# Five raw places and three high places for streamed weight tiles, in place of four and four

## What is computed

```
gate, up = split(rms_norm(h, g_ffn_pre) @ w_ffn_in, 2)            # stack 1
h = h + rms_norm((silu(gate) * up) @ w_ffn_out, g_ffn_post)
x = x + 0.5 * swiglu_ffn(rms_norm(x, ffn1_norm[i]), ffn1_w_in[i], ffn1_w_out[i])   # stack 2
```

## Time and profile before

| | us |
|---|---|
| median of 3 runs | 2286.14 (2285.11 to 2287.39) |
| the profiled execution's own time | 2287.08 |
| its span, first to last instruction | 2285.3 |
| TensorE busy | 2260.3 (99%) |
| TensorE's weight loads | 1985.0 (87%) |
| VectorE busy | 1577.3 (69%) |
| ScalarE busy | 1317.1 (58%) |
| weights' DMA queue, share of 16 engines | 52.5% |

### The profile page before, as it was taken

One profiled execution on the slowest core, in us unless ns is written; L12 is line 12 of the kernel. 1 busy time (PEld: TensorE's weight loads), 2 busy tenths in 40 slices (PEclk: granted clock), 3 DMA queues, 4 the chain that ended last, 5 costly groups with the idle time before them and its releaser, 6 DMA issues.

```text
span 2285.3 us, 31183 instructions
## 1 busy us (share of the span) xinstructions
PE 2260.3 (99%) x13072; PEld 1985.0 (87%) x13072; DVE 1577.3 (69%) x1803; ACT 1317.1 (58%) x1797; POOL 39.0 (2%) x74
## 2 busy tenths in 40 slices
PE   8999999999999999999999999999999999999998
PEld 8898888878988888888898889888888898989886
DVE  6866767478766775667577767675776588667755
ACT  6665655477655655565448745554554558555544
POOL 1000000010000000010000000000100000000000
PEclk9999999999999999999999999999999999999999
DMA  7615555556245655566555355555665655455553
GB/s 227 227 65 184 185 193 188 183 189 231 96 148 184 203 185 193 184 203 193 184 181 178 119 191 191 196 187 186 200 208 177 202 167 166 142 191 183 186 193 120
DMA packets 323515, 411.92 MB, mean 180 GB/s; under 512 B 11600, under 2 KB 245456, under 8 KB 323376
## 3 DMA queue, kind: packets, MB, share of 16 engines
q1 hardware_dynamic: 318160, 394.68, 52.5%
q0 software_dynamic: 4928, 14.26, 2.1%
q10 hardware_dynamic: 288, 0.99, 0.1%
HBM read 408.85 MB, written 1.05 MB: 179 GB/s over the span
## 4 chain that ended last, share of the span: by engine, by line
PE 88%; DVE 5%; ACT 4%; DMA 1%; issue 1%; SPq 0%; DVEq 0%; ACTq 0%
PE banks L610 27%; PE banks L618 14%; PE banks L687 9%; PE banks L689 9%; PE banks L688 9%; PE banks L594 3%; PE banks L595 3%; PE banks L596 3%; DVE lo L1769 2%; ACT hi L1185 1%; DMA raw<-in_w_in 1%; PE banks L738 1%; PE banks L864 1%; PE banks L873 1%; PE banks L841 1%
## 5 line engine op out<-in xcount | busy, mean ns | idle before, releaser
L1769 DVE TENSOR_TENSOR lo<-raw,hi 128x2048 fp32r<-128x2048 f32 (+1 forms) x382 | 858.4, 2250 | 521.9 <-ACT hi L1185 518.0
L1185 ACT ACTIVATE hi<-raw 128x2048 fp32r<-128x2048 f32 (+1 forms) x382 | 715.7, 1878 | 254.3 <-DMA raw<-in_ffn_w_out 84.5
L610 PE MATMUL banks<-x_in,hi 128*128 128x512 f32 x2304 | 537.7, 390 | 0.0
L610 PEld LDWEIGHTS banks<-x_in,hi 128*128 128x128 f32 x2304 | 427.7, 188 | 86.1 <-issue 0.4
L618 PEld LDWEIGHTS banks<-x_in,lo 128*128 128x128 f32 x2304 | 286.5, 192 | 5.8 <-issue 0.2
L618 PE MATMUL banks<-x_in,lo 128*128 128x256 f32 x2304 | 289.3, 283 | 0.0
L594 PE MATMUL banks<-x_in,hi 128*128 128x256 f32 x736 | 210.5, 286 | 0.0
L595 PE MATMUL banks<-x_in,hi 128*128 128x256 f32 x736 | 208.2, 283 | 0.0
L596 PE MATMUL banks<-x_in,lo 128*128 128x256 f32 x736 | 208.2, 283 | 0.0
L687 PE MATMUL banks<-hi,x_hid 128*128 128x512 f32 x528 | 206.0, 390 | 0.0
L689 PE MATMUL banks<-hi,x_hid 128*128 128x512 f32 x528 | 205.5, 389 | 0.0
(11 more groups left out here) (343 smaller groups left out, 3081.0 us busy)
## 6 DMA issues: line engine op xcount, KB each, us to landing
raw<-in_w_in SPq DMA_DIRECT2D x108, 1024.0 KB, 5.1
raw<-in_ffn_w_in SPq DMA_DIRECT2D x88, 1024.0 KB, 5.1
raw<-in_w_ffn_in SPq DMA_DIRECT2D x44, 1024.0 KB, 5.1
raw<-in_ffn_w_out SPq DMA_DIRECT2D x40, 1024.0 KB, 5.1
raw<-in_w_ffn_out SPq DMA_DIRECT2D x20, 1024.0 KB, 5.1
raw<-in_w_o_gla SPq DMA_DIRECT2D x8, 1024.0 KB, 5.2
raw<-in_w_o_attn SPq DMA_DIRECT2D x8, 1024.0 KB, 5.2
raw<-in_w_out SPq DMA_DIRECT2D x8, 1024.0 KB, 5.1
```

The source lines that it names most:

```text
L610: mm = pe.matmul(bank[b + f], wh[:, k, f * P:(f + 1) * P], x[:, k, :, :].rearrange("p n s -> p (n s)"), start=(start and k == 0), stop=(k ...
L1185: act_fn(high, of, ACT.Copy).then_inc(hi_done.up(), 1)
L1769: tt(rest, of, parts(tile, hi)[0].bitcast(F32), ALU.subtract).then_inc(lo_done.up(), 1)
```

## The change

The raw places (with the remainders in them) become five, the high places three, with the same 64 KB together. So a load waits for the tile five before it, and each `hi` index is taken modulo three. ScalarE gets a wait of its own before it writes a high part: for the tile three before to be used. Nothing else moves, and the number of instructions differs only by these waits.

```
-SLOTS = 4
+SLOTS, HIGHS = 5, 3
...
-        o_hi, o_raw = room(SLOTS * 8 * KB), room(SLOTS * 8 * KB)
+        o_hi, o_raw = room(HIGHS * 8 * KB), room(SLOTS * 8 * KB)
...
-        hi = [at(f"hi{i}", [P, TILE], o_hi + i * 8 * KB, F32R) for i in range(SLOTS)]
+        hi = [at(f"hi{i}", [P, TILE], o_hi + i * 8 * KB, F32R) for i in range(HIGHS)]
...
+        def high_slot(tile):
+
+            return place(tile) % HIGHS
...
-                wh = hi[slot(tile)][:, 0:tile.kc * cols].rearrange("p (k n) -> p k n", k=tile.kc)
+                wh = hi[high_slot(tile)][:, 0:tile.kc * cols].rearrange("p (k n) -> p k n", k=tile.kc)
...
                     tile = layer_tiles[0][made[0]]
                     act.wait_ge(*landed(tile))
+                    if place(tile) >= HIGHS:
+                        act.wait_ge(*tile_used.at(tile.index + 1 - HIGHS))
```

More of the change, by code:

```diff
@@ L401, in ranks @@
         def ranks(tile, of, part, twin):
-            dims = of[slot(tile)][:, 0:tile.kc * P].rearrange("p (k d g l r) -> p k d g l r", k=tile.kc, d=2, g=2, l=2)
+            dims = of[place(tile) % len(of)][:, 0:tile.kc * P].rearrange("p (k d g l r) -> p k d g l r", k=tile.kc, d=2, g=2, l=2)
             return dims[:, :, :, twin, part, :]
@@ L421, in parts @@
             if tile.nc >= P:
-                return of[slot(tile)][:, 0:tile.kc * tile.nc], as_loaded(tile)
+                return of[place(tile) % len(of)][:, 0:tile.kc * tile.nc], as_loaded(tile)
             src = as_loaded(tile).rearrange("p (k n) -> p k n", k=tile.kc)
-            return (of[slot(tile)][:, 0:tile.kc * P].rearrange("p (k c n) -> p k c n", k=tile.kc, n=tile.nc),
+            return (of[place(tile) % len(of)][:, 0:tile.kc * P].rearrange("p (k c n) -> p k c n", k=tile.kc, n=tile.nc),
                     src.unsqueeze(2).broadcast_to([P, tile.kc, P // tile.nc, tile.nc]))
@@ L604, in joint_b @@
                 take(b, b + 1)
-                wh = hi[slot(tile)][:].rearrange("p (k n) -> p k n", k=KD)
+                wh = hi[high_slot(tile)][:].rearrange("p (k n) -> p k n", k=KD)
                 wl = lo[slot(tile)][:].rearrange("p (k n) -> p k n", k=KD)
@@ L667, in rows_a @@
             def rows_a(tile, x, to, t, first, last, late=None, turn=None):
-                wh = hi[slot(tile)][:, 0:tile.kc * tile.nc].rearrange("p (k n) -> p k n", k=tile.kc)
+                wh = hi[high_slot(tile)][:, 0:tile.kc * tile.nc].rearrange("p (k n) -> p k n", k=tile.kc)
                 wl = lo[slot(tile)][:, 0:tile.kc * tile.nc].rearrange("p (k n) -> p k n", k=tile.kc)
@@ L792, in ple_rows @@
                     pe.wait_ge(*lo_done.at(tile.index + 1))
-                wh = hi[slot(tile)][:, 0:TILE].rearrange("p (k n) -> p k n", k=2)
+                wh = hi[high_slot(tile)][:, 0:TILE].rearrange("p (k n) -> p k n", k=2)
                 wl = lo[slot(tile)][:, 0:TILE].rearrange("p (k n) -> p k n", k=2)
@@ L893, in low_rank @@
                 take(b)
-                w = hi[slot(tile)][:, 0:tile.kc * P].rearrange("p (k n) -> p k n", k=tile.kc)
+                w = hi[high_slot(tile)][:, 0:tile.kc * P].rearrange("p (k n) -> p k n", k=tile.kc)
                 for k in range(tile.kc):
```

## The result

The changed kernel takes 2303.61 us (median of 4 runs, 2302.31 to 2303.96) where the kernel before took 2285.7 beside it: a ratio of 1.0079, 95% interval 1.0066 to 1.0092. It is slower by 17.9 us. The forecast was 12.6 us slower, 2298.8, with 2303.0 as the upper end of the range; the direction and the places were right, the size of the change was too small by 5.3 us.

The account below looks back on a forecast made before the run. TensorE, busy 2260.3 of 2285.3 us, was taken as the bound. Terms 5.6 + 5.9 + 1.5 - 0.4 = 12.6 us gave a median of 2298.8 us, 0.55% slower, with an 8-in-10 range of 2293.5 to 2303.

Parts of the forecast that it names:

- A: End of block 2's first feed-forward: copy and `xn` 2.74 us later, layer 1 2.84; sum 5.6 us.
- B: End of block 2's `wo`: copy 3.63 us later, TensorE loses 2.96, layer 1 the same; sum 5.9 us.
- C: End of block 1's feed-forward: copy 1.6 us later; two layers cost 1.5 us, between 0 and 3.2.
- steady stretches: Tiles away from the start and row-job ends: copy at most a few tenths later, 6.7 us to spare; cost 0.
- satisfied waits: The further wait instruction in front of 380 copies, when already met: cost 0, upper bound 1 us.
- D: End of block 2's second feed-forward: copy 2.4 us later, repaid in layer 0; -0.4 in the sum, bounds -1.8 and +4.8.
- the passage: From block 1 to 2, where a copy also waited for its transfer: -0.5 to 0, set against `wo` at 0.
- Rival 3: Worse: several places uncovered or at their upper ends and the waits at 1 us; 21 us slower, 2307; chance 0.09.
- wo: Block 1's `wo`: only `lo` comes some 0.3 us later; 0 to 0.6 for both layers, set at 0.
- Rival 4: The queue holds the loads, so they do not come earlier and a repayment of 1.0 goes; 2300; chance 0.08.
- Rival 1: Faster: earlier loads end ScalarE's waits for transfers and shrink TensorE's waits at job ends; 2284.3; chance 0.06.
- rival 2: Half of the loss hidden, as a stall in one place lets others catch up; 6.8 us, or 2293; chance 0.10.

Follow-up runs that it names:

- keep_busy: The changed kernel with 14 and 18 unread identity transposes ahead of TensorE's two long waits, in both layers: 2298.97 us, ratio 1.0060.
- wait_only: The kernel before with four raw places and three high parts, so the new wait without the earlier loads: 2304.05 us, ratio 1.0081.
- both_later: The changed kernel with ScalarE's copy and VectorE's remainder of the second tile after a row job's last moved behind job-end work: 2285.34 us, ratio 0.9999.
- after_a: The changed kernel run once more unaltered, for a second profile: 2303.10 us.
- after: The first profile of the changed kernel (five raw places, three high places), measured at 2303.61 us, ratio 1.0079 against the kernel before.
- act_later: The changed kernel with only ScalarE's copy moved behind the turned copies at the row jobs' ends, VectorE's order kept: 2290.81 us, ratio 1.0023.

## Why the prediction was wrong in size

**Right: the mechanism and the places.** ScalarE stops in front of the copy of last+2, eight times in the program, and what stands behind it is late. The waits that the forecast named came, in the order that it gave: 2.09 us for the turned parts at A (2.2 forecast) and 2.60 for `xn` at B (a loss of 2.96 forecast, 3.05 and 3.04 in `keep_busy`). The late data alone cost 11.8 us at A and B, where the sum had 11.5. C is 1.6 for 1.5. The steady stretches cost nothing. The satisfied waits cost nothing. Shown by `wait_only` (the loss is the high parts') and by `both_later` (it goes when nothing of worth stands behind the wait).

**The step that failed: "2.74 later" and "2.96 lost" as the whole price of A and B.** The sum took a stop of TensorE to cost its own length, and all matmuls after it to run as before. They don't: of the 16.4 us at A and B, 11.8 are late data (`keep_busy`: 2.80 + 2.91 + 3.05 + 3.04) and 4.6 are matmuls at the lower clock. B's stretch is 3.41 us from 1418.59 to 1422.00 at 0.50, and costs 1.5 us; A's costs only 0.8 because TensorE would have waited 0.57 us for `xn` meanwhile. `keep_busy` takes these 4.6 us away without bringing any data earlier. That it lands at 2298.97, on the forecast's 2298.8, is in part luck: over the kernel before beside it, it is 13.6 us slower and not 12.6, and the errors at D and at the passage (next paragraph) partly cancel. The row that would have told me stands in the profile before, behind the 1.81 us of D.

**A second step, hidden in the first comparison: D's repayment of 1.0.** The chain worked as described: after the change the transfer is out early, the copy at 1619.59 is released by TensorE, and TensorE's wait behind it is 0.4 us. But it was priced from one execution whose transfer was late. Against an ordinary one D costs 1.2 us in both layers and gives nothing back, 1.6 more than the -0.4 of the sum. Part of it is offset at the passage from block 1 to 2 (-0.7 for 0), but there too the one execution matters: it is -0.3 against the profile before, and the seven profiles with four and four places differ by up to 0.7 us there. The remark that the profiled run lay 0.9 us above the median was the place to ask which wait made it so; that wait was one of the terms.

**The rivals.** Rival 3 (worse, 2307) was nearest in size but for other reasons: D's 4.8, C's upper end, `wo` at 0.6 and a price for the waits did not come. Rival 4 (the loads do not come earlier) is answered by `wait_only`: early or not, they are worth 0.4 us. Rival 1 falls: ScalarE's waits for weights were off the path, as the forecast said. Of rival 2 nothing was seen: no place was hidden by another.

**What stays open.** Why the clock held at one of six waits of 2.1 us, and why it fell at such different moments after the same wait. And the test of the clock inside the kernel before, since its wait did not come again.

## What to carry to other kernels

In an engine that runs its program in order, a wait costs what stands behind it; before a buffer ring is cut by one, look at which work follows the copy at the ends of jobs, and move it ahead. Here that took the whole loss back, though it cost 0.5 us of its own at each C. A stop of TensorE of about 2 us is to be priced with the slow matmuls after it (0.8 to 1.5 us each here), and work that nobody reads can buy them back. A wait that is to be repaid in the sum must be looked at in more than one execution.

## What the runs showed of the hardware

The granted clock fell to 0.50 at the end of a wait or behind it, each time for about 3.4 us. In twelve falls the moment ranged from 0.4 us before TensorE took up work again (`after_a`, B of layer 1) to 1.5 us after it (`after`, A of layer 0); in `wait_only` it was 0.0 to 1.0 us after, in `after` 0.9 to 1.5. In the fourteen profiles of this study, between the first and the last microseconds of the program, the clock fell so at all six waits of 2.6 us (`after`, `after_a`, `wait_only`), at five of six of 2.1 us, at the one of 1.81 us, and at none of those of 1.7 us and less (1.1 us at 973 in every profile, 1.2 and 1.1 us at A and B in `act_later`, 1.1 to 1.7 us for `lo` near 18.5). One transfer of 1 MB, at the same place in the program, landed 4.8, 4.9, 5.0, 5.3, 5.4, 6.5 and 6.6 us after its issue in seven executions with four and four places.
